# Feed-forward gate and up products: the weight chunk stationary and both token tiles moving, the result made transposed; the row scale as a tile

## The reference

```python
h = rms_norm(x, norm_pre[l, 0])
x = x + 0.5 * rms_norm(swiglu_ffn(h, ffn1_w_gate[l], ffn1_w_up[l], ffn1_w_down[l]), norm_post[l, 0])
...
def swiglu_ffn(h, w_gate, w_up, w_down):
    return (jax.nn.silu(h @ w_gate) * (h @ w_up)) @ w_down
def rms_norm(x, g):
    xf = x.astype(jnp.float32)
    y = xf * lax.rsqrt(jnp.mean(xf * xf, axis=-1, keepdims=True) + NORM_EPS)
    return (y * g.astype(jnp.float32)).astype(x.dtype)
```

## Time and profile before

| | |
|---|---|
| median of three runs | 2399.75 us |
| the profiled execution: its own time | 2404.61 us |
| its span, first to last instruction | 2402.9 us |
| PE busy (matmul) | 2308.1 us, 96% |
| VectorE (DVE) busy | 1755.4 us, 73% |
| ScalarE (ACT) busy | 1405.2 us, 58% |
| mean granted clock of PE | 0.992 of full |
| DMA, mean over the span | 207 GB/s |

### The profile page before, as it was taken

One profiled execution on the slowest core, in us unless ns is written; L12 is line 12 of the kernel. 1 busy time (PEld: TensorE's weight loads), 2 busy tenths in 40 slices (PEclk: granted clock), 3 DMA queues, 4 the chain that ended last, 5 costly groups with the idle time before them and its releaser, 6 DMA issues.

```text
span 2402.9 us, 39540 instructions
## 1 busy us (share of the span) xinstructions
PE 2308.1 (96%) x11130; PEld 1886.4 (79%) x11130; DVE 1755.4 (73%) x2344; ACT 1405.2 (58%) x1892; POOL 235.0 (10%) x296
## 2 busy tenths in 40 slices
PE   9998999999998999999999998999999999999998
PEld 7777788878777788877887777788878877777887
DVE  5777888887778888886556888755565568787555
ACT  5653777774653777774445576454554466665444
POOL 0000000000000000000000790000000019700000
PEclk9999999999999999999999999999999999999999
DMA  7444899985444899995555444465555654444652
GB/s 260 132 140 136 312 336 332 344 327 163 129 144 141 312 335 336 341 328 170 185 188 173 143 149 162 155 219 184 183 187 184 189 158 158 135 164 152 215 183 96
DMA packets 277775, 497.31 MB, mean 207 GB/s; under 512 B 20512, under 2 KB 112848, under 8 KB 277632
## 3 DMA queue, kind: packets, MB, share of 16 engines
q1 hardware_dynamic: 273440, 481.60, 60.1%
q0 software_dynamic: 4192, 14.02, 1.9%
HBM read 494.50 MB, written 1.05 MB: 206 GB/s over the span
## 4 chain that ended last, share of the span: by engine, by line
PE 71%; DVE 13%; DVEq 6%; issue 4%; ACT 3%; DMA 2%; ACTq 1%; PEldq 0%; SPq 0%; PEld 0%; POOLq 0%
PE g_bank L600 14%; PE g_bank L602 14%; PE g_bank L601 14%; PE s_bank L600 8%; PE s_bank L602 8%; PE s_bank L601 8%; DVE w_lo L589 4%; DVE conv_y L2578 2%; PE t_bank L1712 1%; DVEq L2572 1%; ACT w_hi L584 1%; DVEq L2215 1%; PE t_bank L1861 1%; DMA w_raw<-in_moe_w_down_dram 1%; DVE row_max L2239 1%
## 5 line engine op out<-in xcount | busy, mean ns | idle before, releaser
L589 DVE TENSOR_TENSOR w_lo<-w_raw,w_hi 128x1024 fp32r<-128x1024 f32 x929 | 1117.9, 1232 | 376.0 <-ACT w_hi L584 348.4
L584 ACT ACTIVATE w_hi<-w_raw 128x1024 fp32r<-128x1024 f32 x929 | 966.4, 1058 | 437.5 <-PE s_bank L602 190.7
L600 PE MATMUL g_bank<-w_hi,xt_hi 128*128 128x512 f32 (+1 forms) x1152 | 463.2, 402 | 21.7 <-DVEq L652 10.7
L602 PE MATMUL g_bank<-w_hi,xt_lo 128*128 128x512 f32 (+1 forms) x1152 | 451.4, 392 | 0.0
L601 PE MATMUL g_bank<-w_lo,xt_hi 128*128 128x512 f32 (+1 forms) x1152 | 450.8, 391 | 0.0
L600 PEld LDWEIGHTS g_bank<-w_hi,xt_hi 128*128 128x128 f32 x1152 | 219.8, 191 | 78.0 <-issue 21.8
L602 PEld LDWEIGHTS g_bank<-w_hi,xt_lo 128*128 128x128 f32 x1152 | 219.5, 191 | 46.7
L601 PEld LDWEIGHTS g_bank<-w_lo,xt_hi 128*128 128x128 f32 x1152 | 220.2, 191 | 41.3
L600 PE MATMUL s_bank<-w_hi,xt_hi 128*128 128x512 f32 x640 | 252.6, 395 | 0.0
L602 PE MATMUL s_bank<-w_hi,xt_lo 128*128 128x512 f32 x640 | 249.7, 390 | 0.0
L601 PE MATMUL s_bank<-w_lo,xt_hi 128*128 128x512 f32 x640 | 249.4, 390 | 0.0
(11 more groups left out here) (338 smaller groups left out, 2720.7 us busy)
## 6 DMA issues: line engine op xcount, KB each, us to landing
w_raw<-in_w_in_dram SPq DMA_DIRECT2D x192, 512.0 KB, 4.5
w_raw<-in_moe_w_gate_dram SPq DMA_DIRECT2D x128, 512.0 KB, 5.2
w_raw<-in_moe_w_up_dram SPq DMA_DIRECT2D x128, 512.0 KB, 5.5
w_raw<-in_moe_w_down_dram SPq DMA_DIRECT2D x128, 512.0 KB, 5.3
w_raw<-in_ffn_w_gate_dram SPq DMA_DIRECT2D x176, 256.0 KB, 2.9
w_raw<-in_ffn_w_up_dram SPq DMA_DIRECT2D x176, 256.0 KB, 3.1
w_raw<-in_ffn_w_down_dram SPq DMA_DIRECT2D x88, 512.0 KB, 3.4
w_raw<-in_w_branch_dram SPq DMA_DIRECT2D x40, 512.0 KB, 4.5
```

The costliest lines, as they stand in the source:

```text
L584: nc.scalar.activation(half_of(w_hi, u, h), half_of(w_raw, u, h), ACT.Copy).then_inc(hi_ready, 1)
L589: nc.vector.tensor_tensor(half_of(w_lo, u, h), half_of(w_raw, u, h), half_of(w_hi, u, h).bitcast(F32), ALU.subtract).then_inc(lo_ready, 1)
L600: nc.tensor.matmul(dst, a_hi, b_hi, start=first, stop=False)
L602: return nc.tensor.matmul(dst, a_lo, b_hi, start=False, stop=last)
```

## The change

In blocks 1 to 10 the weights are the stationary operand, 128 columns at a time, and both token tiles move, 256 columns. The result has the hidden index on the partitions already. The transposes of these blocks are gone. A block now takes 96 matmuls of 256 columns where it had 48 of 512. Unit 1 of a block is all of gate (8 chunks of 128 rows by 256 columns), unit 2 all of up. PE goes through a unit twice, once for each 128 hidden columns (`ch`), so the first half of a unit is given free after 36 of its 48 matmuls, the second after 48.

The row scale now runs along the free dimension. It becomes a tile `rstd_row`, 128 x 256, the same in every partition, made once for each feed-forward: DVE writes two diagonal matrices, PE multiplies them by a matrix of ones in plain float32 (`rstd_rows`), and DVE copies the result. DVE multiplies gate by it before the silu and silu by it after. `hidden_hi` and `hidden_lo` split the hidden values from SBUF. Block 0 stays as it was, with its transposes.

```diff
+                    def gate_then_up(u, w, j):
+                        for i, name in enumerate(("gate", "up")):
+                            src = d[f"{w}_w_{name}_2"][bass.ds(l, 1), :, bass.ds(j * 256, 256)]
+                            load(u + i, src.rearrange("a (k p) n -> p (a k) n", p=P), 256, 8)
...
+                    def silu_t(q):
+
+                        act.wait_ge(ffn_gate_ready, q.value(1, 1))
+                        act.activation(ffn_silu[:, :, :], ffn_gate[:, :, :], ACT.Silu)
+                        act.drain().then_inc(up_silu_ready, 1)
+
+                    def hidden_hi(q, b):
+
+                        act.wait_ge(ffn_hid_ready, q.value(1, 2))
+                        for k in range(2):
+                            act.activation(ffn_t_hi[:, b, k, :], ffn_hid[:, k, :], ACT.Copy).then_inc(ffn_hi_ready, 1)
...
+                    def block_rest(uj, q):
+                        split_hi(uj, AHEAD + 2)
+                        silu_t(q)
+                        split_hi(uj, AHEAD + 3)
+
+                    def after_down(uj, q):
+                        split_hi(uj, AHEAD + 4)
+                        split_hi(uj, AHEAD + 5)
+                        unit_is_used(act, uj + 2)
+                        hidden_hi(q, 0)
...
+                        for side in sides:
+                            uu = uj + side
                             s = uu.slot(RING)
-                            for h in range(2):
-                                half_is_split(uu, h)
-                                for tt in range(TT):
-                                    for k in (2 * h, 2 * h + 1):
-                                        kk = 4 * half + k
-                                        last = mm3(s_bank[:, tt * 512:(tt + 1) * 512], xt_hi[:, kk, tt * P:(tt + 1) * P],
-                                                   xt_lo[:, kk, tt * P:(tt + 1) * P], w_hi[:, s, k * 512:(k + 1) * 512],
-                                                   w_lo[:, s, k * 512:(k + 1) * 512], kk == 0, kk == 7)
-                                last.then_inc(w_used, 1)
...
+                            for ch in range(2):
+                                c0 = side * 512 + ch * TT * P
+                                for h in range(2):
+                                    if ch == 0:
+                                        half_is_split(uu, h)
+                                    for k in range(4 * h, 4 * h + 4):
+                                        w0 = k * 256 + ch * P
+                                        last = mm3(s_bank[:, c0:c0 + TT * P], w_hi[:, s, w0:w0 + P], w_lo[:, s, w0:w0 + P],
+                                                   xt_hi[:, k, :], xt_lo[:, k, :], k == 0, k == 7)
+                                    if ch == 1:
+                                        last.then_inc(w_used, 1)
...
+                    def rstd_rows():
+
+                        pe.wait_ge(rstd_diag_ready, 2 * l + (w + 1))
+                        for tt in range(TT):
+                            bank = t_wait(t + (4 + tt))
+                            pe.matmul(bank[:, 0:P], c("ones"), rstd_diag[:, tt, :], start=True, stop=True).then_inc(t_ready, 1)
...
                         gate_up(uj, sj)
                         down(uj + 2, qj + -1, False, False)
-                        hid_t(tj, qj)
...
+                    def gate_scaled(uj):
+
+                        unit_is_used(dve, uj)
+                        dve.tensor_tensor(ffn_gate[:, :, :], s_bank[:, 0:512].rearrange("p (a b) -> p a b", a=2), rstd_cols, ALU.mult)
+                        dve.drain().then_inc(ffn_gate_ready, 1)
+
+                    def silu_scaled(q):
+
+                        dve.wait_ge(up_silu_ready, q.value(1, 1))
+                        dve.tensor_tensor(ffn_gate[:, :, :], ffn_silu[:, :, :], rstd_cols, ALU.mult)
+
+                    def hidden_from(uj):
+
+                        dve.drain()
+                        unit_is_used(dve, uj + 1)
+                        dve.tensor_tensor(ffn_hid[:, :, :], s_bank[:, 512:1024].rearrange("p (a b) -> p a b", a=2), ffn_gate[:, :, :], ALU.mult)
+                        dve.drain().then_inc(ffn_hid_ready, 1)
+                        dve.sem_inc(s_free, 1)
+
+                    def hidden_lo(q, b):
+
+                        dve.wait_ge(ffn_hi_ready, q.value(2, 2))
+                        dve.tensor_tensor(ffn_t_lo[:, b, :, :], ffn_hid[:, :, :], ffn_t_hi[:, b, :, :].bitcast(F32), ALU.subtract)
+                        dve.drain().then_inc(ffn_t_ready, 1)
```

More of the change, by code:

```diff
@@ L474, in build @@
         ffn_t_lo = sb("ffn_t_lo", [P, 2, 2, TT * P], F32R, scope=ffn)
+        ffn_gate = sb("ffn_gate", [P, 2, TT * P], scope=ffn)
+        rstd_diag = sb("rstd_diag", [P, TT, P], scope=ffn)
+        rstd_row = sb("rstd_row", [P, TT * P], scope=ffn)
         ffn.close()
@@ L897, in feed_forward @@
                             uj = At(u.const - 1, *u.terms, (j, 3))
-                            gate_up(uj, w, j)
+                            gate_then_up(uj, w, j)
                             down(uj + 2, w, j - 1)
@@ L1228, in feed_forward, with silu @@
                     in_root(i, n, ffn_junk[:, :])
-                    def silu(u_up, q, banks=s_tiles):
+                    def silu(u_up, q, banks):
                         unit_is_used(act, u_up)
@@ L1820, in feed_forward, with gate_up @@
                     q0 = At(w * FB, (l, 2 * FB))
[L1822 to L1823 removed]
+                    def gate_up(uj, sj, sides=(0, 1)):
+                        if sides[0] == 0:
                             s_wait(sj)
[L1825 to L1826 removed]
+                        for side in sides:
+                            uu = uj + side
                             s = uu.slot(RING)
[L1828 to L1838 removed]
@@ L2516, in feed_forward, with hidden @@
                     q0 = At(w * FB, (l, 2 * FB))
-                    def hidden(q, banks=s_tiles):
+                    for tt in range(TT):
+                        dve.tensor_scalar(rstd_diag[:, tt, :], ident, rstd_in[:, tt:tt + 1], None, ALU.mult)
+                    dve.drain().then_inc(rstd_diag_ready, 1)
+                    rstd_cols = rstd_row[:, :].unsqueeze(1).to_broadcast([P, 2, TT * P])
+                    def hidden(q, banks):
                         dve.wait_ge(up_silu_ready, q.value(1, 1))
@@ L2534, in hid_t, with block, after_down @@
                         dve.drain().then_inc(ffn_t_ready, 1)
+                    def gate_scaled(uj):
[15 more added lines that the diff above has]
+                        dve.drain().then_inc(ffn_t_ready, 1)
+                    def block(uj, q):
+                        gate_scaled(uj)
+                        split_lo(uj, AHEAD + 2)
+                        silu_scaled(q)
+                        split_lo(uj, AHEAD + 3)
+                        hidden_from(uj)
+                    def after_down(uj, q):
+                        split_lo(uj, AHEAD + 4)
+                        split_lo(uj, AHEAD + 5)
+                        hidden_lo(q, 0)
                     ahead(u)
@@ L2540, in feed_forward @@
                         dve.sem_inc(g_free[(f + fill).slot(4)], 1)
+                    for tt in range(TT):
+                        tf = t + (4 + tt)
+                        dve.wait_ge(t_ready, tf.value(1, 1))
+                        dve.tensor_copy(rstd_row[:, tt * P:(tt + 1) * P], t_bank[tf.slot(2)][:, 0:P]).then_inc(t_free[tf.slot(2)], 1)
                     ahead(u, 2)
-                    hid_t(t + 4, q0)
-                    ahead(u, 3)
-                    hidden(q0 + 1)
-                    ahead(u, 4)
-                    hid_t(t + 6, q0 + 1)
+                    hid_t(t + 6, q0)
+                    block(u + 2, q0 + 1)
+                    after_down(u + 2, q0 + 1)
                     with dve.Fori(2, FB - 1) as j:
-                        uj, tj, qj = (At(a.const + b, *a.terms, (j, k)) for a, b, k in ((u, -1, 3), (t, 4, 2), (q0, 0, 1)))
+                        uj, qj = (At(a.const + b, *a.terms, (j, k)) for a, b, k in ((u, -1, 3), (q0, 0, 1)))
                         ahead(uj)
-                        ahead(uj, 1)
-                        hidden(qj)
-                        ahead(uj, 2)
-                        hid_t(tj, qj)
+                        block(uj, qj)
+                        after_down(uj, qj)
                     ahead(u, U_FFN - 4)
-                    ahead(u, U_FFN - 3)
-                    hidden(q0 + (FB - 1))
+                    block(u + (U_FFN - 4), q0 + (FB - 1))
+                    hidden_lo(q0 + (FB - 1), 1)
                     split_lo(u + (U_FFN - 2), AHEAD)
-                    hid_t(t + (2 + 2 * FB), q0 + (FB - 1), 1)
                     split_lo(u + (U_FFN - 2), AHEAD + 1)
```

35 lines of the change are left out of this document (15 added, 20 removed).

## The result

The changed kernel takes 2406.51 us (median of 9 runs, 2403.16 to 2408.78); the kernel before took 2399.75 us (9 runs, 2397.74 to 2406.21). The ratio is 1.0021, with a 95% interval of 1.0011 to 1.0031: slower, by 5.0 us with bounds of 2.6 and 7.4 (the medians differ by 6.8). That is small, about 0.2%, but clear of the scatter. The prediction was 2388 us, faster.

The account below looks back on a forecast made before the run. PE's matmul starts were taken to bound the kernel. Transposes -18.0, gate and up +2.4 and `rstd_rows` +3.8 summed to -11.8 us, from 2399.75 to 2388 us, with a range of 2379 to 2405.

Parts of the forecast that it names:

- p = 114: Gate and up: assumed distance in ns between starts of matmuls moving 256 columns over 128 freshly loaded ones.
- +2.4: Gate and up: 96 matmuls at 114 ns against 10.88 us a block, +0.06 us in each of 40 blocks, +2.4 us.
- Rival 1: Gate and up: fixed surcharge on each matmul loading 128 columns, p about 120, sum +11.8 us, 2411.6 us; chance 0.13.
- The two arguments for 114: Gate and up: equal 6% surcharge at 512 and 256 moving columns, and none at half clock, favoured a per-column surcharge.
- The rule that was weighed: Gate and up: N/2.4 + 2.5 ns a matmul, 109.2 at 256 columns, would make this term -16 us instead of +2.4.
- Transposes, -18.0: PE, blocks 1 to 10: 40 sets of four transposes go, 0.45 us each, -18.0 us.
- `rstd_rows`, +3.8: PE, each of four feed-forwards: two plain float32 matmuls at 0.48 us each, +3.8 us.
- Covers: Feed-forward: slack before PE would wait on ring, `s_bank`, hidden values or start; these were costed at nothing.
- 3.8 predicted: `s_bank` in the loop: free at 12.7 us after DVE reads up, wanted at 16.5, cover 3.8 us.
- 0.9 us was expected: Block 10: hidden values ready about 14.2 us, wanted by down at 15.1, cover 0.9 us; a miss costs some tenths.
- p up to 118.3: Gate and up: upper end of the case with jitter as in down, p from 115.8 to 118.3 ns, chance 0.12.

Follow-up runs that it names:

- experiment 1: Kernel without the whole computation, issuing only series of 48 matmuls of many shapes; with 128 stationary columns, 226.7 ns at 512 moving and 119.8 at 256.
- experiment 2: Changed kernel, but gate_up in blocks 1 to 10 uses 48 matmuls moving 512 weight columns, sums not the reference's; 2386.19 us, ratio 0.9944 to the kernel before.
- experiment 3: Changed kernel, but in blocks 2 to 10 `w_hi` is loaded once for both input parts, 512 columns moving, DVE adding the halves; 2403.20 us, ratio 1.0017 to before.
- experiment 4: Kernel of experiment 3, but in block 10 the hidden rows are formed ahead of the last weight split; 2402.78 us, ratio 1.0012 to the kernel before.

## Why the prediction was wrong

- **Where it failed: "I take p = 114, which is near the row with the same moving shape".** The step treated the surcharge as one of the columns moved. Measured p is 119.9 in the kernel and 119.8 alone: 40 x (96 x 0.1199 - 10.88) = +25 us in place of +2.4. Rival 1 had the mechanism and the number (120.1, block 11.53, +26), with a chance of 0.13. The row that was matched had the right moving columns and the wrong stationary ones. Two rows had 128 stationary; the one of them that was limited by moving had 13.4 ns on top.
- **The two arguments for 114 told nothing.** That 226.7/512 and 113.2/256 agree within 0.5% was chance: the first is 213.3 + 13.3 and the second 106.7 + 6.6, two surcharges whose ratio happens to be near 2. That the surcharge is gone at half clock doesn't tell the two kinds apart either. In experiment 1 the series of 256 moving and 96 stationary began at a granted clock of 0.50, at 213 ns a matmul, just 256 columns at 1.2 GHz; when the clock was back at full it ran at about 116, 9 more than 256 columns at 2.4 GHz. So a surcharge can vanish at half clock at this length as at 512.
- **The rule that was weighed.** The Trainium skill (TensorE: Matmul & The Clock Gate, Back-to-back issue gap) gives N/2.4 + 2.5 ns for a single warm matmul by itself. Measured here, in series with a load each, that holds for bfloat16 (109.2 at 256 columns, 215.8 at 512), not for float32r with 128 stationary columns (119.8 and 226.7). Its form, a fixed amount on each matmul, was right where mine was not.
- **Transposes, -18.0: right.** 0.45 us a turn in experiment 2.
- **`rstd_rows`, +3.8: right in kind, twice too large.** 1.8 us. The 32 records of the earlier trace rows are sixteen matmuls of two records each and not eight of four: each of the eight results is summed over both token tiles, and the two matmuls in the changed kernel leave four records.
- **Covers: they held.** PE never waits in the loop. VectorE read up out of `s_bank` from 1158.57 to 1159.26, 3.6 us ahead of its next use at 1162.81 (3.8 predicted). In block 10, where 0.9 us was expected, the changed kernel lost nothing: its 48 matmuls of down take 11.44 us up to the next start, without idle time of PE. Experiments 3 and 4 show how near that was.
- **The sum.** -18.0 + 25 + 1.8 = +8.8 us; the feed-forward sections grew by 8.1, and the medians by 6.8, with an interval of 2.6 to 7.4 from the ratio. The range up to 2405 rested on p up to 118.3 and missed the median by 1.5 us.

## What to carry to other kernels

Take a matmul's price from a row that agrees in both operands and in type: stationary columns, moving columns, float32r or bfloat16. If there is none, measure it in a kernel like that of experiment 1. A ratio of columns hides that halving the moving side doubles the number of surcharges: here 96 x 13.3 ns a turn instead of 48, 0.64 us, more than the 0.45 that four transposes cost. But a straight line is no law either: with 16 stationary columns 128, 256 and 512 moving take 59.9, 113.3 and 231.7 ns, and the first two would put the third at 220. Here the saved transposes would have paid only if the matmuls had stayed as long. And when two profiles are compared, compare the stage that was changed; the clock in the other stages moved the span by 4.7 us, more than half of the 8.1 us of the effect.

## What the runs showed of the hardware that was not expected

- At 512 moving columns a matmul with 16 stationary columns starts every 231.7 ns, one with 128 every 226.7. Less to load was slower. At 256 moving it is the other way round (113.3 and 119.8).
- Down has the shapes of gate_up before the change, and still 232.6 ns; the pair in experiment 3 had 233 + 117 where uniform series gave 226.7 + 119.8. Neither is explained.
- In experiment 1 the granted clock fell to 0.5 in the middle of uninterrupted PE work, behind about 85 us of matmuls without a gap. It fell 2.1 us into the series of 64 moving and 128 stationary columns and came back about 4 us into the series of 256 moving and 96 stationary. PE ran at 213 ns a matmul in both. For the first that is the load, since 64 columns at 1.2 GHz are 53 ns: its pace of 111.7 ns at full clock nearly doubled. For the second it is the columns that move:

```profile
97.30:107.00 9.70, 9.70 (x50) 9.70 (x50) 0.00 (x0) 0.00 (x0) 0.00 (x0) 0.53 0.01 2
108.12:111.48 3.36, 3.36 (x30) 3.36 (x30) 0.00 (x0) 0.00 (x0) 0.00 (x0) 1.00 0.00 0
```

- The first series of experiment 1 (256 moving, 128 stationary), at the beginning of PE's work, also started its matmuls 213 ns apart up to about 15.9 us and 120 ns apart behind it, although the table by stretches gives a clock of 1.00 for both. The distances fit the lower level; the profile's clock doesn't show it. So where the two disagree at the beginning of PE's work, go by the distance.
